# Issuing the second mixer's first value and key products inside the tail of the RWKV stream

## The reference

```python
h = _rmsnorm(x, norm_w)
u = h @ w_in                                   # both mixers read the same h
gq, gk, gv, glr, gg = _split(gla_u, GLA_SPLITS)
log_a = log_sigmoid(glr @ gla_gate_up + gla_gate_bias) / GLA_TAU
o = _gla_chunked(q, k, v, log_a)               # k_in = k*exp(-b), q_in = q*exp(b), b = cumsum(log_a)
gla_out = o * rsqrt(mean(o*o) + eps) * gla_norm_w * silu(gg)
y = _rwkv7_scan(r, decay, k, v, kk, a)         # state carried over all tokens
rwkv_out = (group_norm(y) + bonus) * silu(rg)
x = x + concat([gla_out, rwkv_out]) @ w_out
```

## Time and profile before

| what | value |
|---|---|
| median of 3 runs | 3493.3 us (3489.03 to 3494.76) |
| the profiled execution | 3489.02 us, span 3487.2 us |
| PE busy (modelled) | 3289.8 us, 94% of the span |
| DVE / ACT / POOL busy | 2187.5 / 1461.8 / 563.4 us |
| mean granted TensorE clock | 0.975 of full speed |
| RWKV's last matmul ends, second mixer's first starts | 932.2 us, 937.6 us from the span's start |

### The profile page before, as it was taken

How to read it: one execution, slowest core, us unless ns; L and a number is a source line. 1 busy time by engine, 2 the same in 40 slices (tenths; PEclk the granted TensorE clock), 3 DMA queues, 4 the chain that set the end, 5 groups by cost and what they waited for, 6 DMA issues and landing times. The chain is left out here.

```text
span 3487.2 us, 75240 instructions
## 1 busy us (share of the span) xinstructions
PE 3289.8 (94%) x31246; PEld 2817.5 (81%) x31246; DVE 2187.5 (63%) x3703; ACT 1461.8 (42%) x2121; POOL 563.4 (16%) x792
## 2 busy tenths in 40 slices
PE   7999999999699998989989999959999999999997
PEld 5778878788577886867877878749999999999997
DVE  4666766667554655677787866676555656565563
ACT  5445444444255665332233224424444444444442
POOL 3555555555100000000000000000100110011000
PEclk9999999999999999989999999959999999999999
DMA  4221222211233434422122244446666666666662
GB/s 146 57 83 52 66 75 61 80 51 51 67 127 109 142 113 156 134 85 68 65 73 85 77 157 157 148 137 203 214 209 207 212 205 206 214 199 215 200 217 73
DMA packets 361839, 452.83 MB, mean 130 GB/s; under 512 B 15189, under 2 KB 300149, under 8 KB 361589
## 3 DMA queue, kind: packets, MB, share of 16 engines
q1 hardware_dynamic: 350200, 407.33, 36.0%
q0 software_dynamic: 9216, 33.56, 4.1%
q10 hardware_dynamic: 2176, 8.39, 0.6%
HBM read 382.10 MB, written 67.13 MB: 129 GB/s over the span
## 5 line engine op out<-in xcount | busy, mean ns | idle before, releaser
L2895 PE MATMUL bank<-ex_x_hi,ex_w_lo 128*128 128x256 f32 x2048 | 581.4, 284 | 2.0 <-DVE ex_x_lo L3077 2.0
L2896 PE MATMUL bank<-ex_x_lo,ex_w_hi 128*128 128x256 f32 x2048 | 580.2, 283 | 0.0
L2897 PE MATMUL bank<-ex_x_hi,ex_w_hi 128*128 128x256 f32 x2048 | 580.1, 283 | 0.0
L2891 DVE TENSOR_TENSOR ex_w_lo<-ex_w_loaded,ex_w_hi 128x2048 fp32r<-128x2048 f32 x192 | 433.8, 2289 | 226.7 <-ACT ex_w_hi L2887 222.3
L2887 ACT ACTIVATE ex_w_hi<-ex_w_loaded 128x2048 fp32r<-128x2048 f32 x192 | 359.4, 1904 | 171.7 <-PE bank L2897 169.3
L2895 PEld LDWEIGHTS bank<-ex_x_hi,ex_w_lo 128*128 128x128 f32 x2048 | 393.6, 192 | 2.8 <-issue 2.2
L2896 PEld LDWEIGHTS bank<-ex_x_lo,ex_w_hi 128*128 128x128 f32 x2048 | 393.6, 192 | 0.6
L2897 PEld LDWEIGHTS bank<-ex_x_hi,ex_w_hi 128*128 128x128 f32 x2048 | 393.7, 192 | 0.0
L2338 PE MATMUL bank<-sc_tokens_hi,sc_w_lo 128*128 128x512 f32 x672 | 266.9, 397 | 28.6 <-DVE hidden_hT_split L2468 12.5
L2951 POOL CAST ex_idx<-kept_masks 128x2 uint32 (+1 forms) x16 | 3.0, 186 | 1735.7 <-POOLq L79 1424.7
L2340 PE MATMUL bank<-sc_tokens_hi,sc_w_hi 128*128 128x512 f32 x672 | 264.6, 394 | 0.0
(11 more groups left out here) (498 smaller groups left out, 8303.2 us busy)
## 6 DMA issues: line engine op xcount, KB each, us to landing
ex_w_loaded<-in_wg SPq DMA_DIRECT2D x64, 1024.0 KB, 5.4
ex_w_loaded<-in_wu SPq DMA_DIRECT2D x64, 1024.0 KB, 6.2
ex_w_loaded<-in_wd SPq DMA_DIRECT2D x64, 1024.0 KB, 5.1
plain_weights<-in_w_in SPq DMA_DIRECT2D x70, 512.0 KB, 4.7
gl_ada_tile<-in_ada_w SPq DMA_DIRECT2D x48, 512.0 KB, 4.4
plain_first_w<-in_sc_w_in SPq DMA_DIRECT2D x24, 1024.0 KB, 5.2
plain_columns<-hT_dram SPq DMA_DIRECT2D x14, 1024.0 KB, 7.5
plain_columns<-in_x SPq DMA_DIRECT2D x16, 512.0 KB, 5.7
```

The source lines that it names most:

```text
L2891: nc.vector.tensor_tensor(w_lo[c % SPLIT][:], raw[:, c % LOADED, :], w_hi[c % SPLIT][:].bitcast(F32), ALU.subtract).then_inc(s["lo"], 1)
L2895: nc.tensor.matmul(psum, ll, rh, start=first, stop=False)
L2896: nc.tensor.matmul(psum, lh, rl, start=False, stop=False)
L2897: return nc.tensor.matmul(psum, lh, rh, start=False, stop=last)
```

## The change

The products v0, v1 and k of unit 0 are taken out of the second mixer's PE list and issued by `fill` in slots 32, 33 and 34 of the RWKV stream, by a new function `gla_product`. They go to banks 4, 5 and 2 (`GLA_AHEAD`), in which the second mixer's ACT and DVE read them. In slot 32 v0 is cut in pieces of 4, 3, 3, 3 and 3 groups of 3 matmuls, one at each `fill`; v1 is cut likewise in slot 33; k is cut in 2, 2, 2, 1 and 1 blocks in slot 34. A piece of part 4 stands ahead of `turn_y`. No DMA and no ACT or DVE instruction is added, taken away or moved within its queue. The turns in the two banks are counted without the three products.

```diff
+        def gla_in(i, half, part):
+            g = 2 * i + half - 3
+            if not NG <= g < NG + 3:
+                return None, range(0)
+            return ("v0", "v1", "k")[g - NG], range(*((0, 4, 7, 10, 13, 16) if g < NG + 2 else (0, 2, 4, 6, 7, 8))[part:part + 2])
...
+                def gla_product(name, groups):
+                    h_hi, h_lo = [whole[:, 1, :].rearrange("p (kb t) -> p kb t", t=QT) for whole in (cols_buf.hi, cols_buf.lo)]
+                    if 0 in groups:
+                        pe.wait_ge(s["next_lo"], 7 if name == "k" else 6)
+                        if name == "k":
+                            pe.wait_ge(s["gh_kept"], NG)
+                        else:
+                            pe.wait_ge(s["t"], 2 * NG * LEVELS)
+                    for m in groups:
...
+                        for p, (stationary, moving) in enumerate(ops):
+                            mm = nc.tensor.matmul(psum, stationary, moving, start=(kb == 0 and p == 0), stop=(kb == KD - 1 and p == 2))
+                        if m == (7 if name == "k" else 15):
+                            mm.then_inc(s["gla"], 1)
...
+                    gla_product(*gla_in(i, half, part))
                     if half == 1 and part == 4:
...
                     fill(i, half, 4)
+                pe.wait_ge(s["gla"], 3)
...
+GLA_AHEAD = {("v0", 0): 4, ("v1", 0): 5, ("k", 0): 2}
...
-        job, before = {}, []
+        job, before = {key: -1 for key in GLA_AHEAD}, []
...
-                    n = len(job)
+                    n = len(before)
...
                     pe.wait_ge(s["state"], 8 * c + 1)
+                    if c == 0:
+                        pe.wait_ge(s["v_kept"], 2)
...
-                    values(u, 0)
+                    if u:
+                        values(u, 0)
...
-                    values(u, 1)
+                    if u:
+                        values(u, 1)
...
-                    block_product(u, "k")
+                    if u:
+                        block_product(u, "k")
...
-            psum_of = lambda *key: bank[RB[job[key] % 2]]
+            psum_of = lambda *key: bank[GLA_AHEAD[key] if key in GLA_AHEAD else RB[job[key] % 2]]
...
-                    act.wait_ge(s["job"], job[(f"v{part}", u)] + 1)
+                    wait_for(act, s["job"], job[(f"v{part}", u)] + 1)
...
-                    dve.wait_ge(s["job"], job[("k", u)] + 1)
+                    wait_for(dve, s["job"], job[("k", u)] + 1)
```

More of the change, by code:

```diff
@@ L122, in rwkv @@
             "x", "x_kept", "wu", "wu_kept", "gh", "q_part", "gh_kept", "state_mm", "state", "y_in", "y_first", "y", "y_kept",
-            "next_h", "next_v", "next_k", "next_hi", "next_lo", "centred", "ysq", "yvar", "ysd", "ynorm", "out", "stored"])
+            "next_h", "next_v", "next_k", "next_hi", "next_lo", "centred", "ysq", "yvar", "ysd", "ynorm", "out", "stored", "gla"])
         xts, h_los, h_his = [[whole[:, i, :].rearrange("p (n d) -> p n d", d=D) for i in range(2)] for whole in (cols_buf.x, cols_buf.lo, cols_buf.hi)]
@@ L292, in turn_y @@
                     mm.then_inc(s["job"], 1)
+                def gla_product(name, groups):
[7 more added lines that the diff above has]
+                    for m in groups:
+                        if name == "k":
+                            hi, lo = [whole[:, 2 * D + m * P:2 * D + m * P + P] for whole in (cols_buf.w_hi, cols_buf.w_lo)]
+                            ops, psum, kb = ((lo, h_hi[:, m, :]), (hi, h_lo[:, m, :]), (hi, h_hi[:, m, :])), k.bank[GLA_AHEAD["k", 0]], m
+                        else:
+                            n, kb = divmod(m, KD)
+                            ts = slice((2 * int(name[1]) + n) * P, (2 * int(name[1]) + n + 1) * P)
+                            hi, lo = [whole[:, kb * 2 * P:kb * 2 * P + 2 * P] for whole in (cols_buf.w_hi, cols_buf.w_lo)]
+                            ops, psum = ((h_lo[:, kb, ts], hi), (h_hi[:, kb, ts], lo), (h_hi[:, kb, ts], hi)), k.bank[GLA_AHEAD[name, 0]][:, n * 256:n * 256 + 256]
+                        for p, (stationary, moving) in enumerate(ops):
+                            mm = nc.tensor.matmul(psum, stationary, moving, start=(kb == 0 and p == 0), stop=(kb == KD - 1 and p == 2))
+                        if m == (7 if name == "k" else 15):
+                            mm.then_inc(s["gla"], 1)
                 def fill(i, half, part):
```

## The result

| | before | after |
|---|---|---|
| median of 14 runs each | 3489.64 us (3485.06 to 3494.76) | 3498.91 us (3491.77 to 3501.71) |
| ratio after / before | | 1.0024, 95% interval 1.0016 to 1.0032 |
| the profiled execution, its span | 3489.02, 3487.2 us | 3501.24, 3499.5 us |

The change makes the kernel slower by 0.24%, 8.4 us by the ratio (5.6 to 11.2); the two medians lie 9.3 us apart. The forecast was +6.4 us and 3499.7 us; the three runs shown beforehand had a median of 3493.3, 3.7 us above that of the fourteen, so part of the agreement of the absolute number is luck, and the rise was forecast 2 us too small.

The account below looks back on a forecast made before the run. Unit 0 was taken to be bound by a chain through ACT, DVE and queries, not by PE; from the median, 7.5 - 4.0 + 2.0 + 0.9 = +6.4 us gave 3499.7 us, range 3493.5 to 3504.5.

Parts of the forecast that it names:

- What bounds unit 0: Unit 0: PE does not bound it, so v1 and k taken out of it gain nothing there.
- the chain: Sets unit 0's end: v0, lr, z, ACT's gate, weight splits, adaLN tiles, queries, g1, lr of unit 1.
- Rival B1: Unit 0: PE bounds it, so all work that leaves counts; -11.7 us, 3481.6 us; chance 0.08.
- Term A: Tail of the RWKV stream, slots 32 to 34: the moved products make it longer, +7.5 us (+7.2 to +10.6).
- Term B: Start of the second mixer's phase: lr starts sooner, 3.8 us in instead of 7.8; -4.0 us.
- Term C: Start of the phase: lr begins at half clock after PE idles 9 us; +2.0 us (0 to +2.2).
- Term E: g1 in unit 0: a longer PE wait may halve the clock; +1.7 us against the profile, +0.9 against the median.
- the sign that the prediction named for it, 0.50 at g1: Unit 0: the granted clock would read 0.50 at g1 in the profile after.
- The sum: Whole kernel: +7.2 us against the profiled execution (3496.2), +6.4 from the median (3499.7, 0.18% slower).
- B2: Slot 32: the clock falls inside the tail, v1 begins at half clock; +9.1 us, 3502.4 us; chance 0.20.
- B3: The clock holds throughout, at lr and at g1; +3.5 us, 3496.8 us; chance 0.10.

Follow-up runs that it names:

- experiment 1: Against the kernel before, only part of the products moved: v0 in slot 32, ratio 1.0016; v1 and k, 1.0023; v0 whole in slot 33, 1.0008.
- experiment 2: The whole change, with DVE's queries ahead of adaLN tiles 2 to 4 in unit 0; ratio 1.0009 against the kernel before.

## Why the prediction was right

**What bounds unit 0.** Right, and shown: v1 and k lay beside the chain (experiment 1), the chain was held by queries behind the adaLN tiles (experiment 2). Rival B1 (-11.7 us) is out.

**Term A,** forecast +7.5, measured +8.2 against the profiles in which the clock holds in slots 30 to 32, and +7.1 against the two in which it falls. The mis-sized part is slot 32: I took 3.1 us where 3.3 was the sum and 3.9 is the measure. I had discounted 0.2 us because a queue that stays full would save start-ups. It went the other way: cut in five pieces, v0 took 6.6 us and not 5.9. v1 and k gave +4.3, where I had 4.4. PE instead of the norm was late, by 4.9 us: the transposes start at 945.52, DVE's norm had ended at 940.61 (forecast 5).

**Term B,** forecast -4.0: lr's low part ends 3.7 us into the phase in both kernels (954.98 + 0.23 - 951.54), and lr starts right then. Right.

**Term C,** forecast +2.0 (0 to 2.2), measured 1.4 to 2.6 by the throwaway matmuls. In the profile of after it was 2.7: from lr's start to ACT's copy it took 8.5 us, and 5.8 before. As forecast, lr began at half clock behind a gap of 9 us. The advice of the Trainium skill ("TensorE: Matmul & The Clock Gate", section "Why this matters for your kernels") to leave no long gap between bursts agrees with the trace: with PE supplied in the wait, lr had its full clock. But the filler has to stand where the gap is, behind the barrier, and not ahead of it. The prediction was wrong to say that by the rule alone C would be 0: the rule is about every gap, and the change leaves this one of 9 us.

**Term E,** forecast 0 to 1.7, half of it taken: 1.6 where it comes. In the profile of after it did not come, and the sign that the prediction named for it, 0.50 at g1, failed. PE's wait was 3.7 us, not 4.5 or "over 4": g0 ended 35.1 us into the phase where the forecast puts it at about 34, because q began 0.8 us late and ran at half clock for longer, while g1 came only 0.5 us later than forecast (38.8). The reason given for taking half, that the kernel before pays it in some executions, was right (one profile of five).

**The sum.** Within tail and unit 0: forecast +7.2 against the profiled execution, measured +6.6 (A 0.7 more, C 0.7 more, E 1.7 less, and 0.3 less in the rest of the unit). Against the median: forecast +6.4; the traces give +6.1 against the mean of the five profiles of before, and the runs +8.4 (5.6 to 11.2). So the parts are accounted for, and some 2 us of the measured rise lie outside the tail and unit 0, where the prediction had put nothing and no experiment found a cause. I gave the most chance to a rise under 0.2%; 0.24% is just over it, and its interval takes in both sides.

**B2** (the clock falls inside the tail): it did not, neither in this profile nor in the two others with the whole tail; at 921.5 to 951.5 the mean clock was 0.99. **B3** (it holds throughout) is out: lr ran at 0.50.

## What to carry to other kernels

Work moved into an idle stretch is free only up to the wait that it stands under: v0 under the norm cost nothing that the traces can tell, the same v0 a slot earlier cost 3.9 us, and what follows it, being longer than the wait, delayed the phase by 4.3 more. Work taken out of a stretch gains nothing where the engine already waits at its end; look first for the wait that ends last there (here 2.7 us for a reader that stood behind three prefetched tiles) and cut that. Idle time in PE's row says where work fits, not where it is worth anything.

## What the runs showed of the hardware

The granted clock falls not only over long idle time. In slot 30, which is mostly 64x64 matmuls, it fell to half in 11 of 14 profiles, although PE never stood still for more than 1.6 us at a time in it or in the 12 us ahead of it. A slot with the clock at 1.00 took 17.3 to 17.4 us and one with a fall 19.6 to 21.0. A stall of 2.5 to 2.75 us ahead of g1 kept the clock in four profiles and lost it in three, at 1.6 us. Two profiles of the same kernel before differ by up to 9.3 us in span (3482.3 and 3491.6: 4.9 us ahead of the seam, 2.5 in tail and unit 0, 1.9 after them), which is more than the effect that was studied: a term is better compared stretch by stretch, and the clock of each stretch read beside it.
